# Twenty-eight products of constants in two waits of TensorE: one inference step of a two-layer hybrid decoder

## What is computed

```python
def hier_moe(h, w_r1, b_r1, w_r2, b_r2, w_gate, w_up, w_down):
    xt = h.reshape(B * T, D)
    g_prob = jax.nn.softmax((xt @ w_r1).astype(F32) + b_r1, axis=-1)
    p_grp, grp = lax.top_k(g_prob, 1)                     # one of 4 groups
    e_all = jnp.einsum('nd,gde->nge', xt, w_r2).astype(F32) + b_r2
    e_logit = jnp.take_along_axis(e_all, grp[:, :, None], axis=1)[:, 0]
    p_e, e_idx = lax.top_k(jax.nn.softmax(e_logit, axis=-1), TOP_IN_GROUP)   # two of 4 experts
    p_e = p_e / jnp.sum(p_e, -1, keepdims=True)
    expert = grp * EXPERTS_PER_GROUP + e_idx
    gate = jnp.zeros((n, N_EXPERTS), F32).at[jnp.arange(n)[:, None], expert].add(p_grp * p_e)
    hid = jax.nn.silu(jnp.einsum('nd,edf->nef', xt, w_gate)) * jnp.einsum('nd,edf->nef', xt, w_up)
    y = jnp.einsum('nef,efd->nd', hid * gate[:, :, None].astype(hid.dtype), w_down)
```

## Time and profile before

| | us |
|---|---|
| median of three timed runs | 2596.89 |
| lowest and highest | 2591.98, 2602.91 |
| the profiled execution, its time | 2585.08 |
| its span, first to last instruction | 2583.2 |
| mean granted TensorE clock in it | 0.948 of 2.4 GHz |

### The profile page before, as it was taken

How to read it: one execution, slowest core, us unless ns; L and a number is a source line. 1 busy time by engine, 2 the same in 40 slices (tenths; PEclk the granted TensorE clock), 3 DMA queues, 4 the chain that set the end, 5 groups by cost and what they waited for, 6 DMA issues and landing times.

```text
span 2583.2 us, 31839 instructions
## 1 busy us (share of the span) xinstructions
PE 2351.4 (91%) x12343; PEld 1432.2 (55%) x12343; DVE 637.6 (25%) x1157; ACT 511.6 (20%) x1126; POOL 61.1 (2%) x60
## 2 busy tenths in 40 slices
PE   6899999999498989898989998999994999999997
PEld 4678775688233434343568875545872343434344
DVE  0259911500622121212210000032016112121213
ACT  1220116400510101010220015633014110101004
POOL 0000000000300000000000000000004000000000
PEclk9999999999779999999989999989996899999998
DMA  8523457864029898989735356998430598989890
GB/s 272 175 97 132 164 155 250 256 247 163 0 109 417 357 417 353 417 345 417 255 103 163 139 171 215 365 327 292 166 131 0 233 416 359 418 354 418 355 372 34
DMA packets 251063, 647.65 MB, mean 251 GB/s; under 512 B 56825, under 2 KB 90250, under 8 KB 216890
## 3 DMA queue, kind: packets, MB, share of 16 engines
q1 hardware_dynamic: 215578, 636.28, 65.1%
q10 hardware_dynamic: 35376, 9.91, 1.7%
HBM read 640.16 MB, written 5.96 MB: 250 GB/s over the span
## 4 chain that ended last, share of the span: by engine, by line
PE 76%; DMA 12%; ACT 4%; DVE 3%; ACTq 2%; issue 1%; POOL 1%; SPq 0%; POOLq 0%; DVEq 0%
PE bank L599 17%; PE bank L1073 11%; PE bank L1183 9%; PE bank L1057 8%; PE bank L1103 7%; DMA ring<-in_w_down 6%; DMA ring<-in_w_up 5%; PE bank L1117 5%; PE bank L777 4%; PE bank L786 2%; PE bank L917 2%; ACT arena L1204 2%; ACTq L379 1%; PE bank L988 1%; PE bank L898 1%
## 5 line engine op out<-in xcount | busy, mean ns | idle before, releaser
L1073 PE MATMUL bank<-ring,AT 128*64 128x512 f32 x2048 | 455.8, 604 | 27.3 <-DMA ring<-in_w_up 25.5
L1204 ACT ACTIVATE arena<-bank 128x512 f32<-128x512 f32 (+6 forms) x571 | 283.4, 546 | 980.5 <-PE bank L599 414.5
L599 PE MATMUL bank<-X,ring 128*128 128x264 f32 x1664 | 373.5, 388 | 1.2 <-ACT arena L1204 1.2
L599 PEld LDWEIGHTS bank<-X,ring 128*128 128x128 f32 x1664 | 317.7, 191 | 56.1 <-ACT arena L1204 1.4
L1073 PEld LDWEIGHTS bank<-ring,AT 128*64 128x64 f32 x2048 | 147.9, 139 | 326.5 <-issue 291.2
L1103 PE MATMUL bank<-ring,arena 128*64 128x512 f32 x1024 | 237.1, 620 | 39.5 <-DMA ring<-in_w_down 29.5
L1057 PE MATMUL bank<-arena 128*128 128x256 bf16 (+1 forms) x1440 | 213.2, 294 | 20.9 <-POOL arena L550 20.9
L1183 PE MATMUL bank<-AT,ring 128*128 128x264 f32 x1024 | 231.5, 390 | 0.0
L1183 PEld LDWEIGHTS bank<-AT,ring 128*128 128x128 f32 x1024 | 196.8, 192 | 34.1
L1891 DVE TENSOR_TENSOR X<-bank,X 128x264 f32<-128x264 f32 x256 | 110.8, 433 | 406.7 <-PE bank L1117 403.7
L1057 PEld LDWEIGHTS bank<-arena 128*128 128x128 bf16 (+1 forms) x1440 | 120.0, 101 | 118.5 <-issue 80.9
(11 more groups left out here) (252 smaller groups left out, 1438.8 us busy)
## 6 DMA issues: line engine op xcount, KB each, us to landing
ring<-in_w_gate SPq DMA_DIRECT2D x64, 2048.0 KB, 17.5
ring<-in_w_up SPq DMA_DIRECT2D x64, 2048.0 KB, 13.3
ring<-in_w_down SPq DMA_DIRECT2D x64, 2048.0 KB, 16.6
ring<-in_w_o SPq DMA_DIRECT2D x16, 2048.0 KB, 9.9
ring<-in_cache_b_k SPq DMA_DIRECT2D x128, 256.0 KB, 4.2
ring<-in_cache_b_v SPq DMA_DIRECT2D x128, 256.0 KB, 4.9
ring<-in_w_in_a SPq DMA_DIRECT2D x14, 2048.0 KB, 9.2
ring<-in_w_in_b SPq DMA_DIRECT2D x12, 2048.0 KB, 8.3
```

The costliest lines, as they stand in the source:

```text
L599: mm = pe.matmul(B[4 * (g % 2) + f][:, 0:n_tok], u[:, c * 512 + f * P:c * 512 + (f + 1) * P], src[8 * half + c][:, 0:n_tok], start=(half = ...
L1073: mm = pe.matmul(B[bank][64 * s:64 * s + 64, :], M.xsT[:, at:at + 64], ring[slots[s][0]][:, c * FE:(c + 1) * FE], start=(half == 0 and c = ...
L1204: return act.activation(out, in_, ACT.Copy, scale=scale)
```

## The change

A helper `idle_products(n)` issues n f32 products of 128 by 128 constants (all ones) with the first 512 columns of the table of constants, into bank 1. Nothing reads the result. It is called with 18 ahead of the wait for `chosen`, and with 10 ahead of the wait for `low_made`, in both layers.

```diff
@@ -992,6 +992,11 @@
+            def idle_products(n):
+
+                for _ in range(n):
+                    pe.matmul(B[1][:, :], cst("ones"), consts[:, 0:512], start=True, stop=True)
+
             def router_weights(layer):
@@ -1029,6 +1034,7 @@
                 mm.then_inc(S("logit_rows"), 1)
                 token_rows(range(2), False)
 
+                idle_products(18)
                 pe.wait_ge(S("chosen"), layer + 1)
                 sel = M.w16[0]
                 for t in range(4):
@@ -1040,6 +1046,7 @@
                                        start=(g == 0), stop=(g == min(t, 2)))
                 mm.then_inc(S("ranks"), 1)
                 token_rows(range(2, 3), False)
+                idle_products(10)
                 pe.wait_ge(S("low_made"), cnt["token_rows"])
                 pe.wait_ge(S("zeroed"), ZERO[2] if layer == 0 else ZERO[4])
                 def gather(done):
```

## The result

The changed kernel took 2554.26 us in the median of four runs (2552.82 to 2571.74), the kernel before 2594.43 beside it (2590.10 to 2602.91). The ratio is 0.9855, with a 95% interval of 0.9812 to 0.9898. The profiled execution is the slowest of the four, 2571.74 us; the other three took 2552.8 to 2555.2. That spread is the first lead: one execution in four looks like the forecast (13 us less than the profiled one before), three gained more than even the rival "the clock stands in both gathers" had given.

The account below looks back on a forecast made before the run. TensorE was taken as the bound, its gathers slowed by the half clock after idle waits. Sure part 2.0 us plus one quick gather of two, 11.1, gave 13.1 less: 2596.9 − 13.1 = 2583.8 us, range 2568 to 2598.

Parts of the forecast that it names:

- the clock stands in both gathers: Second case, a rival: both layers' gathers run at full clock, 24.2 us less, 2572.7 us; chance 0.28.
- What bounds the kernel: TensorE, busy 91% of 2583.2 us; two waits per layer stay, the half clock costs the gathers 22.2 us together.
- The price of a product: One added product of 512 columns on TensorE: 0.88 us at the full clock, 1.76 at half.
- The first 18: Products before the wait for the choice: 17.8 us, with 4 us at half clock, ending at about 697.7.
- The rank products and the sure part: Rank products in 2.4 instead of 4.35 us; the GpSimd chain starts 1.0 us earlier a layer, between 0.5 and 3.
- The last 10: Products before the wait for the low parts: 8.8 us, leaving about 2.5 us idle before the gather, between 1.2 and 3.
- I give each gather an even chance: Whether the clock survives the 2.5 us left idle before each layer's gather: even odds, so one of two counted, 11.1 us.
- The value of a quick gather: Gather at 19.05 us instead of 33.99 and 26.39: 14.9 and 7.3 us saved, mean 11.1 each.
- I count every microsecond of the gather at full value: The expert loop starts as a whole when the gather ends, so a shorter gather, 22.2 us in both layers, counts in full.
- The third rival: The idle time left before the gather costs the clock nearly every time: only 2.0 us gained, 2594.9 us; chance 0.26.
- The case on the other side: The added products themselves become the wait before the rank products and gather: 45 us slower in all, 2642 us; chance 0.08.
- The range: Kernel time 2568 to 2598 us, reaching to both neighbouring rivals with their spreads, without the slower case.

Follow-up runs that it names:

- the doubled run: 36 in place of 18 products before the choice, against the changed kernel: median 2629.6 us, ratio 1.0137 to the kernel before.
- r2_first_only: The changed kernel without the 10 products before the low parts, only the 18 before the choice: median 2586.6 us, ratio 0.9978 to the kernel before.
- r1_same: The changed kernel run once more, unaltered, with 18 and 10 products: median 2554.6 us, ratio 0.9860 to the kernel before.
- r4_18_13: 13 in place of 10 products before the low parts, against the changed kernel: median 2561.2 us, ratio 0.9883 to the kernel before.
- r7_norm: The changed kernel plus four products before each layer's router product and before layer 1's forget gates' product: median 2585.7 us, ratio 0.9967 to the kernel before.
- r9_norm_12: The changed kernel plus four products in the norm's waits, and 12 in place of 10 before the low parts: median 2569.9 us, ratio 0.9905.

## Why the prediction was wrong, and where it was right

**What bounds the kernel, and that the clock is the lever: right.** The two waits stayed, and what moved was the clock in and behind them. The quick gathers took 19.11 us in the changed kernel's traces, near the 19.05 that was read in the loop.

**The price of a product: right.** 0.85 us measured in the doubled run, 0.88 forecast.

**The first 18: right.** Forecast 17.8 us, measured 17.27 and 16.89. The clock was cold at their start and back 3.4 and 2.6 us later; 4 had been taken.

**The rank products and the sure part: right, a little small.** 2.37 us, forecast 2.4. From the end of the transposes before the wait to the gather it took 34.3 us in both layers before and takes 32.9 and 32.5 now: 1.5 and 1.8 us, where 1.0 was taken and 3 was the bound.

**The last 10: the frame was right, the likely case chosen wrongly.** Left idle without the dip: 3.17 us, forecast 2.5 and at most 3. With it: 1.48, where my lower bound had been 1.2 "if the clock dips among the rank products". That sentence named the case that then held, by the times, in nearly every execution; it hangs on a coincidence of a few tenths of a microsecond, told above, that nothing in the prediction could foresee. I had it as the edge of a range because no row of before could show a dip: there the clock was low through the rank products anyway.

**"I give each gather an even chance": this is the step that failed.** With 2.5 us I placed the left-over between the loop's long and short waits. It is never 2.5: it is 3.2, and then the gather was cold in all eight cases of the traces (3.17 to 3.21), or about 1.5, and then it was quick in ten of eleven (1.46 to 1.50). By the times of both measurements some 19 of 20 gathers of the changed kernel stood: its usual case is two quick gathers, where the sum had counted one. The Trainium skill (TensorE: Matmul & The Clock Gate, "Why this matters for your kernels"), which advises against idle gaps above about 3 us, has the long cases right; the single 1.46 us gap that lost the clock is outside its advice, so staying below 3 us is no guarantee in these runs.

**The value of a quick gather was too small: the term of the sum that was mis-sized.** I took 11.1 us each, from the 33.99 and 26.39 us of one trace. The fourteen cold gathers of all traces average 32.3, and behind a cold one the loop's first quad is often slower: 109.8 and 110.0 us in r2_first_only, 108.2 and 108.1 in r1_same. The reason is in the change's own trace: the first gate_up takes 22.54 us behind the cold gather and 20.82 behind the quick one. That is 13.2 us a gather and 1.7 behind it where the clock comes back only in the loop. It does not always: in the kernel before's trace it was back by the end of both cold gathers, and its first quads took 108.5 and 108.2 us with a gate_up of 20.82. Over all traces the first quad averages 109.8 behind the 14 cold gathers and 108.7 behind the 20 quick ones, 1.1 us.

**"I count every microsecond of the gather at full value", and nothing of the loop: half right.** The quick gather did start the loop earlier by what it saved. But the loop was not the same afterwards. r1_same and r2_first_only differ by 38.1 us: 30.4 in the two gathers, 3.5 in the two first quads, 3.1 in the other six, 1.2 before the gathers. Some of the loop's waits lose the clock and some do not, up's at 1.4 to 1.7 us each, and which do differs from trace to trace; what decides it is not shown. It also explains the slow first quads of r4_18_13, at least in part: behind a down wait's fall that both kernels have, it alone shows 8.78 for 7.09 us at up's wait.

**The rivals.** The second, both gathers quick, had the mechanism, at 24.2 us. With the sizes measured since it becomes 3.3 + 2 × (13.2 + 1.1) = 31.9 us, and from the median of 2594.4 that gives 2562.5. The measured 2554.3 is 8 lower; 3 of those may be the loop's falls, as r1_same and r2_first_only differ in them, and the rest of the medians' difference I can't place. Two single executions can be set side by side in full: the spans of the kernel before and of r1_same, 2583.2 and 2551.2 us, differ by 32.0, of which 22.2 lie in the two gathers, 5.1 before them, 0.3 in the first quads and 4.5 in the other six. The prediction's 22.2 for this one profiled execution was exact; what the sum lacked there is 4.8 us of the loop, which it had put at nothing, and 3.1 of the 5.1 before the gathers, where it had 2.0; of the 5.1, however, 2.2 lie ahead of the change's first products, where the two kernels do the same work. The third rival, that the left-over costs the clock nearly every time, is what the traces show at 3.2 us, and not at the 1.5 that was usually left. The case on the other side did not come, and the doubled products showed its slope, 0.85 us each, with both gathers lost on top.

**The range was wrong** because both quick gathers were priced from a trace in which one cold gather was short, 26.39 us, and set against the median, which was 11.8 us slower than that execution. I saw that gap and explained it with nothing. The short gather would account for 7.9 of it against one of 34.3 us; no second trace of the kernel before shows what its slower executions did.

## What to carry to other kernels

Where a stretch of a busy engine is slow because a wait ahead of it cost the clock, fill the wait's end, not its beginning: ten products next to the gather brought 33 us, eighteen ahead of them 6. Leave as little idle time as the chain behind allows (of the traced gathers 0.6 us failed in none of four, 1.5 in one of eleven, 3.2 in eight of eight), but do not fill past it (13 products with the dip cost 6.6 us over 10), and look at single executions, since a median near 2554 hid a 2571.7. And when a fit works, check what it rests on: here a faster router product ahead of it cost 30 us.

## What the runs showed of the hardware that I had not expected

The half clock is sticky for this gather: cold gathers stayed at 1.2 GHz for their whole 34.3 us in six of the fourteen cases, though TensorE was busy throughout, while the f32 products of constants were back at 2.4 GHz some 3 us after they began (678.3 to 681.7 above). No gather of the traces that was at the full clock 2 us after its start lost it afterwards.

A stretch of busy work can lose the clock, and whether it does can hang on a few tenths of a microsecond. The rank products and the transposes behind them run without a gap; the clock fell among these transposes when it had been back for 13.7 to 13.9 us at the start of the rank products, and not at 13.0 or at 14.1. That is how four products in an earlier wait could take the dip away (r1_same, r7_norm), and how one execution could differ between its own two layers. I have not shown why it is so. What decides between keeping and losing the clock at 1.46 us (r9_norm_12) stays open too.
